# A transformer block and a Mamba/xLSTM/mixture-of-experts block on one core: routing rows split unscaled, one native gate, other filler counts

## What is computed

```python
h2 = rmsnorm_2(x, norm2_w)
def hier_moe(h, wg, bg, we, be, w_gate, w_up, w_down):
    # top-1 of 4 groups, then top-2 of its 8 experts; gate = p(group) * softmax(top-2 logits)
    ...
    xs = xf[tok]                                  # 512 token-expert pairs sorted by expert
    hg = lax.ragged_dot(xs, w_gate, sizes)
    hu = lax.ragged_dot(xs, w_up, sizes)
    ys = lax.ragged_dot(jax.nn.silu(hg) * hu, w_down, sizes)
    ys = ys * gates.reshape(-1)[order][:, None]
    y = jax.ops.segment_sum(ys, tok, num_segments=t)
```

## Time and profile before

| | |
|---|---|
| median of 3 executions | 1089.3 us (1088.65 to 1092.28) |
| profiled execution, its own time | 1092.85 us |
| its span in the trace | 1090.8 us |
| TensorE busy | 95% |
| VectorE, ScalarE busy | 78%, 61% |
| mean granted TensorE clock | 0.987 of full speed |
| HBM read | 251.4 MB, 231 GB/s over the span |

### The profile page before, as it was taken

One profiled execution on the slowest core, in us unless ns is written; L12 is line 12 of the kernel. 1 busy time (PEld: TensorE's weight loads), 2 busy tenths in 40 slices (PEclk: granted clock), 3 DMA queues, 4 the chain that ended last, 5 costly groups with the idle time before them and its releaser, 6 DMA issues.

```text
span 1090.8 us, 14945 instructions
## 1 busy us (share of the span) xinstructions
PE 1039.1 (95%) x5602; PEld 881.2 (81%) x5602; DVE 846.5 (78%) x1086; ACT 665.1 (61%) x803; POOL 33.0 (3%) x40
## 2 busy tenths in 40 slices
PE   8999999999989899989888899999999999999997
PEld 7778999999889777879778778777787877878775
DVE  5855766766767556777666889989999999999977
ACT  5554655455545645456333777777777777777764
POOL 1000000000000100100020000000000000000000
PEclk9999999999989999999999899999999999999999
DMA  9634555646424443233310789898898989889981
GB/s 348 239 116 135 193 179 170 216 154 210 160 78 154 161 140 129 78 117 116 117 32 7 288 284 387 349 373 342 363 378 351 389 352 378 361 352 376 364 323 41
DMA packets 82709, 253.59 MB, mean 232 GB/s; under 512 B 4160, under 2 KB 42176, under 8 KB 62656
## 3 DMA queue, kind: packets, MB, share of 16 engines
q1 hardware_dynamic: 82624, 252.50, 61.7%
HBM read 251.44 MB, written 1.05 MB: 231 GB/s over the span
## 4 chain that ended last, share of the span: by engine, by line
PE 71%; DVE 13%; ACT 7%; issue 5%; POOL 1%; DVEq 0%; POOLq 0%; ACTq 0%
PE bank L1852 20%; PE bank L1854 20%; PE bank L1853 20%; DVE WL L983 5%; ACT WH L521 4%; PE bank L2361 4%; DVE CV L1276 1%; PE bank L2343 1%; PE bank L2311 1%; POOL sm L1811 1%; ACT CV L712 0%; PE bank L2176 0%; ACT HTH L543 0%; DVE MXL L1536 0%; PE bank L1858 0%
## 5 line engine op out<-in xcount | busy, mean ns | idle before, releaser
L983 DVE TENSOR_TENSOR WL<-raw,WH 128x2048 fp32r<-128x2048 f32 x234 | 501.8, 2175 | 110.8 <-ACT WH L521 110.7
L521 ACT ACTIVATE WH<-raw 128x2048 fp32r<-128x2048 f32 x234 | 425.4, 1824 | 100.2 <-PE bank L1854 79.7
L1852 PE MATMUL bank<-WH,MXH 128*128 128x512 f32 x552 | 219.2, 397 | 1.6 <-DVE CV L1276 0.9
L1854 PE MATMUL bank<-WH,MXL 128*128 128x512 f32 x552 | 215.9, 391 | 0.0
L1853 PE MATMUL bank<-WL,MXH 128*128 128x512 f32 x552 | 215.6, 391 | 0.0
L1852 PE MATMUL bank<-HTH,WH 128*128 128x256 f32 x576 | 166.6, 289 | 6.4 <-DVE WL L983 3.1
L1853 PE MATMUL bank<-HTL,WH 128*128 128x256 f32 x576 | 164.2, 285 | 0.0
L1854 PE MATMUL bank<-HTH,WL 128*128 128x256 f32 x576 | 164.1, 285 | 0.0
L1852 PE MATMUL bank<-WH,HTH 128*128 128x512 f32 x348 | 139.2, 400 | 6.0 <-DVE HTL L1006 2.4
L1853 PE MATMUL bank<-WL,HTH 128*128 128x512 f32 x348 | 136.3, 392 | 0.0
L1852 PEld LDWEIGHTS bank<-WH,MXH 128*128 128x128 f32 x552 | 104.4, 189 | 22.8 <-issue 1.7
(11 more groups left out here) (382 smaller groups left out, 1106.0 us busy)
## 6 DMA issues: line engine op xcount, KB each, us to landing
raw<-in_exp_w_gate SPq DMA_DIRECT2D x52, 1024.0 KB, 8.2
raw<-in_exp_w_up SPq DMA_DIRECT2D x52, 1024.0 KB, 8.0
raw<-in_exp_w_down SPq DMA_DIRECT2D x52, 1024.0 KB, 6.9
raw<-in_w_in SPq DMA_DIRECT2D x34, 1024.0 KB, 5.1
raw<-in_w_up SPq DMA_DIRECT2D x22, 1024.0 KB, 5.2
raw<-in_w_down SPq DMA_DIRECT2D x11, 1024.0 KB, 4.9
raw<-in_w_out SPq DMA_DIRECT2D x8, 1024.0 KB, 4.9
raw<-in_w_o SPq DMA_DIRECT2D x4, 1024.0 KB, 5.5
```

The costliest lines, as they stand in the source:

```text
L521: e.activation(WH[i % HL][:, 0:n], raw[i % RAW][:, 0:n], ACT.Copy).then_inc(a_wh, 1)
L983: e.tensor_tensor(l, r, h.bitcast(F32), ALU.subtract).then_inc(v_wl, 1)
L1852: e.matmul(out_, ah, bh, start=start, stop=False)
L1854: return e.matmul(out_, al, bh, start=False, stop=stop)
```

## The change

- Routing: `X` is split for the gather without the inverse root, in four half rows (`rows_high` on ScalarE, `rows_low` on VectorE), three of them ahead of the logits' use and one behind the picks. The squares for the norm are taken in halves (`half_squares`). The inverse root joins later: in the token gates (`g1`), and, as a 33rd column of the gate matrix, in the scale of Silu (`rsS`, and `norm_column` for each unit).
- The gather's first half runs over the first 128 tokens for all eight banks and then over the other 128; `SEL` is signalled per token half there. The gate columns `xcols[0]` lie in `WH`/`WL` instead of `MXH`/`MXL`.
- Unit 0's gate is made of 8 native float32 products on `raw` and `XST`; its pieces aren't split. Its up pieces are loaded first and split. `split_count` keeps the counts right.
- Group pick: one step fewer between the index and the masked logits.
- `"n1"`: the first token half's mean is formed before the last `add_to_x`. The two instructions on the residual rows `X` stand behind the convolution of pieces 1 and 2.
- `warm`: 18 becomes 9; 5, 5, 4 become 5, 2, 3; 14, 6, 4 become 21, 3, 3; 20 and 36 stay.

```diff
+def is_native(i):
+
+    return NP <= i < NP + 2
+
+
+def split_count(i):
+
+    return i + 1 - min(max(i + 1 - NP, 0), 2)
...
-        xcols = [[v[:, o:o + 4, :] for v in vs] for vs, o in (((MXH, MXL), 4), ((HTH, HTL), 0))]
+        xcols = [[v[PI["we", 1, 0] % HL][:, 0:4 * S].rearrange("p (k s) -> p k s", k=4) for v in (WH, WL)],
+                 [v[:, 0:4, :] for v in (HTH, HTL)]]
...
             def load_piece(i, src):
                 if i >= RAW:
-                    e.wait_ge(p_used if is_mixed(i - RAW) else v_wl, i - RAW + 1)
+                    j = i - RAW
+                    e.wait_ge(*((p_used, j + 1) if is_mixed(j) or is_native(j) else (v_wl, split_count(j))))
...
-                for w in (a["exp_w_gate_2"], a["exp_w_up_2"]):
+                ws = [(a["exp_w_gate_2"], i), (a["exp_w_up_2"], i + 2)]
+                for w, j in ws if u else reversed(ws):
                     for kh in range(2):
-                        load_piece(i, dyn(w, u, 4 * kh, 4))
-                        i += 1
+                        load_piece(j + kh, dyn(w, u, 4 * kh, 4))
                 if u:
-                    load_down(u - 1, i)
+                    load_down(u - 1, i + 4)
...
                 if i >= HL:
-                    e.wait_ge(p_used, i - HL + 1)
+                    j = i - HL
+                    e.wait_ge(p_used, (j - HL if is_native(j) else j) + 1)
...
+            def half_squares(c, t):
+                e.wait_ge(v_xa, X_ADDS[f"we{c}", t])
+                e.wait_ge(a_sq, SQ["n2", c, t] - 1)
+                e.activation(cvf[:, 0:512], X[:, t, c * 512:(c + 1) * 512], ACT.Square,
+                             accum_out=(ssh, ss)[c][:, t:t + 1]).then_inc(a_sq, 1)
+
+            def rows_high(c, t):
+                x, h = row_halves(H2H, t, c)
+                e.activation(h, x, ACT.Copy).then_inc(a_rh, 1)
+
+            e.wait_ge(p_used, PI["wm1", 1] + 1)
+            for t in range(T):
+                half_squares(0, t)
+                rows_high(0, t)
             x_columns(0, 0)
             x_columns(0, 1)
-            for t in range(T):
-                x_columns(1, t)
-                e.wait_ge(v_xa, X_ADDS["we1", t])
-                e.wait_ge(a_sq, SQ["n2", t] - 1)
-                e.activation(cvf, X[:, t, :], ACT.Square, accum_out=ss[:, t:t + 1]).then_inc(a_sq, 1)
+            half_squares(1, 0)
+            x_columns(1, 0)
+            x_columns(1, 1)
+            half_squares(1, 1)
+            rows_high(1, 0)
+            rows_high(1, 1)
             e.wait_ge(p_sp, 2)
             e.activation(TMP[0:36, 1, 0:256], bank[4][0:36, 0:256], ACT.Copy).then_inc(a_sptv, 1)
-            for t in range(T):
-                e.wait_ge(g_rstd, RSTD["n2", t])
-                m = e.activation(in_rows(H2H[:, t, :]), by_row(X[:, t, :]), ACT.Copy, scale=rs[:, t:t + 1])
-            m.then_inc(a_route, 1)
             e.wait_ge(v_route, V_ROUTE["ge2"])
             e.activation(ge2, ge2, ACT.Exp).then_inc(a_route, 1)
             e.wait_ge(v_route, V_ROUTE["dm"])
             e.activation(dm, dm, ACT.Exp).then_inc(a_route, 1)
-            split(NP)
-            split(NP + 1)
+            split(NP + 2)
+            split(NP + 3)
...
+            def norm_column(u):
+                e.activation(rsu[u % 2], rsS[:, bass.ds(tile[u], 1)], ACT.Copy).then_inc(a_rsu, 1)
+
...
+            split(NP + 4)
             e.wait_ge(p_used, NP + 2)
-            e.activation(SG[0], bank[GU[0][0]][:, :], ACT.Silu).then_inc(a_sg, 1)
-            split(NP + 4)
+            e.wait_ge(v_gm, 2)
+            e.activation(SG[0], bank[GU[0][0]][:, :], ACT.Silu, scale=rsS[:, 0:1]).then_inc(a_sg, 1)
+            norm_column(1)
...
+                e.wait_ge(a_rsu, u)
+                e.activation(SG[u % 2], bank[GU[u % 2][0]][:, :], ACT.Silu, scale=rsu[u % 2]).then_inc(a_sg, 1)
...
+            e.wait_ge(a_sq, SQ["n1", 0])
+            e.tensor_scalar(part[5], ss[:, 0:1], EPS / D, EPS * EPS, ALU.mult, ALU.add).then_inc(own.up(), 1)
+            e.wait_ge(a_sq, SQ["n1", 1])
+            chained(rs[:, 0:1], part[0], 1.0 / D, part[5]).then_inc(v_ms, 1)
             e.wait_ge(p_used, PI["down", NG - 1] + 1)
...
-            for t in range(T):
+
+            def residual(t):
+
                 e.wait_ge(g_rstd, RSTD["fin", t])
                 e.scalar_tensor_tensor(out=X[:, t, :], in0=X[:, t, :], scalar=r1[:, t:t + 1], in1=gb, op0=ALU.mult,
                                        op1=ALU.mult)
...
                 conv("xbc", c, (6, 7) if c % 2 else (4, 5))
+                if 0 < c < 3:
+                    residual(c - 1)
...
+            def rows_low(c, t):
+                e.wait_ge(a_rh, 2 * c + t + 1)
+                (x, h), (_, l) = row_halves(H2H, t, c), row_halves(H2L, t, c)
+                e.tensor_tensor(l, x, h.bitcast(F32), ALU.subtract).then_inc(v_rl, 1)
+
             for t in range(T):
                 x_add("we0", t, 4 + t, 0, PI["we", 0, 1])
+                rows_low(0, t)
             for t in range(T):
                 x_columns(0, t)
             x_add("we1", 0, 6, 1, PI["we", 1, 1])
+            x_add("we1", 1, 7, 1, PI["we", 1, 1])
             x_columns(1, 0)
-            x_add("we1", 1, 7, 1, PI["we", 1, 1])
             row_mean(0)
             x_columns(1, 1)
             row_mean(1)
+            rows_low(1, 0)
...
-            top1(L[:, :, 0:4], 4, const("iota", 4), gmx, goh)
-            e.tensor_tensor(ge2, L[:, :, 0:4], bt(gmx, 4), ALU.subtract).then_inc(v_route, 1)
-            after()
-            e.tensor_scalar(goh, goh, 1.0, 1e30, ALU.subtract, ALU.mult).then_inc(own.up(), 1)
-            after()
-            for t in range(T):
+            eq, idx = first_largest(L[:, :, 0:4], 4, const("iota", 4), gmx)
+            for t in range(T):
+                e.tensor_scalar(goh[:, t, :], eq[:, t, :], idx[:, t, :], -1e30, ALU.subtract,
+                                ALU.mult).then_inc(own.up(), 1)
+            for t in range(T):
+                e.wait_ge(own.sem, own.n - 1)
                 e.tensor_tensor(el[:, t, :].rearrange("p (g c) -> p g c", g=4),
                                 L[:, t, 4:36].rearrange("p (g c) -> p g c", g=4),
                                 bc(goh[:, t, :].unsqueeze(2), P, 4, 8), ALU.add).then_inc(own.up(), 1)
+            e.tensor_tensor(ge2, L[:, :, 0:4], bt(gmx, 4), ALU.subtract).then_inc(v_route, 1)
...
-            e.wait_ge(a_route, A_ROUTE["h2h"])
-            for t in range(T):
-                m = e.scalar_tensor_tensor(out=in_rows(H2L[:, t, :]), in0=by_row(X[:, t, :]), scalar=rs[:, t:t + 1],
-                                           in1=in_rows(H2H[:, t, :].bitcast(F32)), op0=ALU.mult, op1=ALU.subtract)
-            m.then_inc(v_route, 1)
+            rows_low(1, 1)
...
-                m.then_inc(v_sel, 1)
+                    if half == 0:
+                        m.then_inc(v_sel, 1)
+                if half:
+                    m.then_inc(v_sel, 1)
...
+            e.tensor_tensor(g1, g1, rs, ALU.mult).then_inc(own.up(), 1)
+            e.tensor_copy(GX[:, :, 32:33], rs.unsqueeze(2)).then_inc(own.up(), 1)
+            e.wait_ge(own.sem, own.n - 1)
...
+            e.wait_ge(p_route, P_ROUTE["gates"])
+            bg = bank[6][:, 0:33 * NT].rearrange("p (a b) -> p a b", a=NT)
+            e.tensor_tensor(GM, bg[:, :, 0:32], EQg, ALU.mult).then_inc(v_gm, 1)
+            e.tensor_copy(rsS, bg[:, :, 32]).then_inc(v_gm, 1)
+            e.wait_ge(v_gm, 1)
...
-            warm(18, 0)
+            warm(9, 0)
...
             warm(5, 0)
             norm_columns("ffn", 0, (6, 7, 4, 5))
-            warm(5, 0)
+            warm(2, 0)
             norm_columns("ffn", 1, (6, 7, 4, 5))
-            warm(4, 0)
+            warm(3, 0)
...
-            warm(14, 7)
+            warm(21, 7)
             norm_columns("n1", 0, (4, 5, 6, 7))
-            warm(6, 0)
+            warm(3, 0)
             norm_columns("n1", 1, (4, 5, 6, 7))
-            warm(4, 0)
+            warm(3, 0)
...
-            logits(0)
+            logits(0, 0, 1)
             turn_x(1, 1)
-            logits(1).then_inc(p_sp, 1)
+            logits(0, 1, 4)
+            logits(1, 0, 4).then_inc(p_sp, 1)
...
-            for half in range(2):
-                e.wait_ge(v_sel, half + 1)
-                hs = slice(half * (NS // 2), (half + 1) * (NS // 2))
+            e.wait_ge(v_rl, 4)
+            for t in range(T):
+                e.wait_ge(v_sel, t + 1)
                 for k in range(8):
-                    if half == 0 and k == 0:
-                        e.wait_ge(v_route, V_ROUTE["h2l"])
-                    if half:
-                        e.wait_ge(a_xst, k + 1)
-                    for t in range(T):
-                        for i, part in enumerate((H2H, H2L)):
-                            m = e.matmul(bank[GATB[k]][:, 0:NS // 2], part[:, t, k * 128:(k + 1) * 128], SEL[:, t, hs],
-                                         start=(t == 0 and i == 0), stop=(t == 1 and i == 1))
```

(33 more changed lines are left out.)

87 lines of the change are left out of this document (42 added, 45 removed).

## The result

The changed kernel takes **1082.69 us** (median of 5 runs, 1080.93 to 1084.62) against 1091.74 for the kernel before (5 runs, 1088.65 to 1094.91): a ratio of **0.9919, with a 95% interval of 0.9892 to 0.9946**. That is 9.05 us less, by the interval 5.9 to 11.8; forecast were 9.15 us less, and 1080 us. The spans of the two profiled executions differ by more, 1090.8 against 1079.1 us, which is 11.7. Where the 2.7 us by which the spans differ more than the medians come from is the main question of what follows.

The account below looks back on a forecast made before the run. TensorE's own work bounds the unit loop, so gains come only ahead of it: 0.5 + 2.3 + 0.5 + (4.3 + 2.6 - 1.4 - 0.1 + 0.45) = 9.15 us, giving 1080 us, range 1076.5 to 1085.

Parts of the forecast that it names:

- "n1": Norm near 300 us: no idle time, no clock fall, second transposes earlier; 2.3 us, bounds 0.5 and 2.5.
- Start and "ffn": Fewer fillers at the start, worth nothing, and between the "ffn" norm's transposes, 0.5 us.
- The low outcome: At "n1" the clock falls nevertheless, so only the six fewer filler records are won: 0.5 us.
- Convolution: Residual moved behind the splits, TensorE's 3.09 us gap gone, only wait and small instructions won: 0.5 us, bounds 0 and 1.2.
- The gather's start: Routing: half rows, one pick step less and earlier `SEL` start the gather 4.3 us earlier, about 601.7 instead of 605.99.
- The clock in the gather: Gather's first products: idle time ahead falls to about 1.5 us, clock stays up; 2.6 us won, bounds 0 and 2.8.
- the rival: The clock falls in the gather after all: 2.6 us lost, 1082.7 us; chance 0.14.
- The native gate: Unit 0: 16 native records take 6.9 us against 5.47 in split form; costs 1.4 us, at most 2.1.
- `gate_hidden` and the 33rd column: Unit 0: `gate_hidden` done 0.45 us sooner; the gate matrix's 33rd column costs 0.1 us.
- The loop: Loop over units: `norm_column` copies cost nothing; rival that they slow it by 13.5 us, to 1093.7, chance 0.04.
- The weights: Rival: unit 1's weights come late behind the native pieces, losing up to 3 us, 1083 us; chance 0.07.
- The rival on chance: Part of the gather clock rival (chance 0.14): the same idle time may trip the clock in one execution, not the next.

Follow-up runs that it names:

- second batch: The changed kernel unaltered, timed and profiled again beside the next kernels: 1081.93 us (6 runs), ratio 0.9912.
- experiment 7: Changed kernel with "n1" fillers back at 14, 6, 4, run twice: 1085.71 and 1086.66 us; with the first mean also back late: 1087.17 us.
- experiment 2: Changed kernel with both residual instructions back ahead of the first convolution piece: 1081.72 us, ratio 0.9919.
- experiment 3: Changed kernel with 28 instead of 36 filler pairs: 1083.61 us; with all low half rows between picks and counts: 1085.96; the latter with 64 pairs: 1085.29.
- experiment 4: Kernel before with 56 instead of 36 filler pairs ahead of the gather, nothing else: 1090.56 us against 1090.6, ratio 0.9986.
- experiment 6: Changed kernel with each unit's column of norms copied four times in a row on ScalarE: 1081.42 us, ratio 0.9917.

## Why the prediction was right

**The sum.** 9.05 us measured, 9.15 forecast. Of the 11.7 us between the two profiles, 9.8 lie in sections with a forecast term and 1.9 in the other two, where they can't be told from chance. With 2.1 instead of 2.85 us for "n1" and the convolution in some executions, 9.1 to 9.8 are to be expected in the medians; measured are 9.05, and in the second batch 8.92 (1081.93 against 1090.85). That forecast and measurement agree to 0.1 us is luck: the interval is 5.9 us wide. The time of 1080 us was missed by 2.7, and 2.4 of that is the starting point: the forecast subtracted from a median of three runs, 1089.3, and with two runs more the kernel before has 1091.74.

**Start and "ffn"**, 0.5: the first filler of "n1" comes at 294.10 to 294.70 in twelve executions with the new fillers, at 294.94 and 295.04 in those of before: 0.6 in the mean. No run undid these fillers alone.

**"n1"**, 2.3 with the bounds 0.5 and 2.5: 2.19 in the profile. The step was right for the execution I read, but it took a draw for a rule. The second group began at 300.86 - 294.24 = 6.62 us behind the first filler. The low outcome was priced at 0.5 and held for a failure of the change; in fact it depends on the kernel before, whose clock stays up in some executions, and it is worth 0.9 (experiment 7).

**Convolution**, 0.5: 0.66, and 0.5 by experiment 2.

**The gather's start**, 4.3: 4.35. Inside it the half row cost 1.08 instead of 1.0, and a high half row on ScalarE 1.16 instead of 1.05. That the counts' products hide it was only half true: the copy at 587.60 stands right behind the half row, and the products ended at 587.17, so up to 0.4 us of it are exposed. Of the 4.35, 2.8 are the rows' place (experiment 3); the remaining 1.5, ScalarE's half rows, the pick step and the earlier `SEL` signal, were not taken apart.

**The clock in the gather**, 2.6: gather 12.06 to 9.46, exactly 2.60. The rows of before didn't decide whether 1.5 us is short enough. Nine executions with 1.27 to 1.57 us of idle time ahead of it all kept the clock, so the rival is out for this place. But the reason I gave, that both pauses in the rows were longer, doesn't carry: the length of the last pause alone doesn't decide. Between 517 and 524 us the clock fell in all 14 executions, behind pauses of 1.3 and 0.9 us. In the changed kernel TensorE was busy 1.46 of the 3.7 us before that fall, whereas 8.26 us of fillers without a gap stand ahead of the gather's pause:
```profile
515.00:518.70 3.70, 1.46 (x9) 1.03 (x8) 3.11 (x10) 0.62 (x2) 1.67 (x1) 1.00 0.50 192
518.70:522.00 3.30, 3.30 (x9) 2.56 (x8) 2.54 (x5) 2.73 (x4) 0.00 (x0) 0.50 0.02 5
```
What I also hadn't seen is that 0.7 of the term was lost again ahead of unit 1 where the two gate splits still stood (experiment 4).

**The native gate**, -1.4 with 16 records in 6.9 us: 6.87, and 1.40 dearer than 5.47. By the Trainium skill's four passes for three ("FP8 and Floating Point Precision", TensorE Precision Notes) it would have been 7.3; the measurement decides for 6.87, and the difference of 0.4 was rightly not taken.

**`gate_hidden` and the 33rd column**, 0.35: 0.63. The 20 products of the gate matrix last 2.32 us with it and came out free, and the wait of 0.45 is gone. The rest of the 0.63 is that the transposes' records now overlap those before them.

**The loop**, 0: confirmed by experiment 6. **The weights**: no idle time ahead of unit 1, so not late.

**The rival on chance.** The prediction cited the Trainium skill ("TensorE: Matmul & The Clock Gate", The HAM clock gate) for a monitor window that runs freely, and said that profile and median could differ by it. The runs agree: behind the same pause of 2.40 us between 560 and 568 the clock fell in 3 of 13 executions, behind 1.96 us at "n1" in 2 of 3, behind a pause of 1.43 us that ends between 384 and 389 in 8 of 14. The differences by profile and by median did differ, by 2.7 us; 1.0 of it lies in the section where the falls vary, 0.9 in the loop with its slow units.

## What to carry to other kernels

Before a term is read from two profiles, take a second profile of the same program and compare section by section, from mark to mark: here one program's spans differed by 4.4 us, half of the whole gain, while the sections that the change touched repeated within 0.02 us. A filler that keeps the clock up pays only as far as the next engine behind TensorE is ready: here 1.85 us were left of 2.57, so look at that engine's work too. And a pause that lowers the clock in one execution may not in the next: cost it as a chance.

## What was not expected of the hardware

- Between 360 and 520 us the clock falls at partly different places in executions of the same program (low at 388 in one, at 396 and 412 in the other), behind idle times of 0.8 to 2.5 us, and not behind the same ones in the next. Near 519 it fell in every one of 14.
- Three filler products fewer at 300 us went with a stop of 2.5 to 2.8 us near the end (1055 to 1060), which the profile puts to "issue" and in which one instruction transfer lies, in three executions of three. The medians of these kernels are 3.8 to 5.2 us above the changed kernel's for 0.5 to 2.2 us at "n1".
- Single units of the loop take 17.4 to 18.2 instead of 17.19 us, none to five in an execution, mostly at other units each time.
